# Stick-breaking attention in a decoder trunk: another order of the head loop, and the entry copies on VectorE

## The reference, cut to what matters

```python
def sb_block(q, k, v, q_pos, k_pos, bias):
    z = jnp.einsum('bqhd,bkhd->bhqk', q.astype(F32), k.astype(F32)) * (SB_HEAD_DIM ** -0.5)
    z = z + bias.astype(F32)[None, :, None, None]
    mask = k_pos[None, :] < q_pos[:, None]
    lb = jnp.where(mask, jax.nn.log_sigmoid(-z), 0.0)
    rev = lax.cumsum(lb, axis=3, reverse=True)
    after = jnp.concatenate([rev[..., 1:], jnp.zeros_like(rev[..., :1])], axis=-1)
    wgt = jnp.where(mask, jnp.exp(jax.nn.log_sigmoid(z) + after), 0.0)
    return jnp.einsum('bhqk,bkhd->bqhd', wgt, v.astype(F32)).astype(v.dtype)
```

## Time and profile before

| | |
|---|---|
| median of 3 executions | 2492.19 us (2490.45 to 2493.6) |
| the profiled execution | 2492.66 us, its span 2490.6 us |
| TensorE busy | 93% of the span |
| VectorE, ScalarE, GpSimd busy | 65%, 34%, 17% |
| span of stage A's projections and head loop | 425 to 745 us |
| chain that ended last, by engine | TensorE 70%, VectorE 14%, ScalarE 6%, GpSimd 4% |

### The profile page before, as it was taken

The page is one execution under the profiler, slowest core; times in us unless marked ns, Lnnn a source line. Parts: engine busy times, 40 slices in busy tenths (PEclk is TensorE's granted clock), DMA queues, the critical chain, the costliest instruction groups (busy, mean ns, idle before and its releaser), DMA issues.

```text
span 2490.6 us, 45870 instructions
## 1 busy us (share of the span) xinstructions
PE 2314.0 (93%) x18817; PEld 2209.6 (89%) x18817; DVE 1628.9 (65%) x1912; ACT 854.0 (34%) x1050; POOL 423.2 (17%) x323
## 2 busy tenths in 40 slices
PE   5999999986879999999999999989898977999998
PEld 5999999874559999999999999979787867999998
DVE  5666575677865757566757566777777758757573
ACT  5333232214333323234423233443433324423233
POOL 2000003590003000003000004061525264000002
PEclk8999999996889999999999999989999998999999
DMA  3242425572522142424142424243333322142422
GB/s 111 66 114 85 117 70 177 145 219 70 180 77 68 53 120 76 114 81 115 53 127 75 116 80 116 69 119 89 107 102 94 98 85 79 54 125 75 115 80 77
DMA packets 412887, 248.56 MB, mean 100 GB/s; under 512 B 12658, under 2 KB 387802, under 8 KB 412688
## 3 DMA queue, kind: packets, MB, share of 16 engines
q1 hardware_dynamic: 412279, 246.28, 34.7%
q10 hardware_dynamic: 460, 0.20, 0.0%
HBM read 232.48 MB, written 14.61 MB: 99 GB/s over the span
## 4 chain that ended last, share of the span: by engine, by line
PE 70%; DVE 14%; ACT 6%; POOL 4%; issue 3%; DMA 2%; SPq 1%; ACTq 0%; DVEq 0%; POOLq 0%
PE PS L239 45%; PE PS L744 16%; POOL prod L1133 2%; DVE wl L216 2%; PE PS L1344 2%; ACT wh L212 2%; PE PS L1291 1%; DVE xcs L2304 1%; PE PS L1224 1%; PE PS L2109 1%; DVE rstd L303 1%; DVE cbuf L1500 1%; PE PS L1235 1%; DVE xcs L2486 1%; DVE hl L285 1%
## 5 line engine op out<-in xcount | busy, mean ns | idle before, releaser
L239 PE MATMUL PS<-hh,wh 128*128 128x260 f32 (+1 forms) x2512 | 518.9, 288 | 33.2 <-DVE hl L285 12.8
L239 PE MATMUL PS<-hh,wl 128*128 128x260 f32 (+1 forms) x2512 | 510.6, 285 | 0.0
L239 PE MATMUL PS<-hl,wh 128*128 128x260 f32 (+1 forms) x2512 | 510.0, 285 | 0.0
L216 DVE TENSOR_TENSOR wl<-raw,wh 128x2048 fp32r<-128x2048 f32 (+2 forms) x187 | 345.0, 1845 | 153.8 <-ACT wh L212 152.4
L239 PEld LDWEIGHTS PS<-hh,wh 128*128 128x128 f32 (+1 forms) x2512 | 392.1, 191 | 47.5 <-issue 35.1
L239 PEld LDWEIGHTS PS<-hl,wh 128*128 128x128 f32 (+1 forms) x2512 | 391.7, 190 | 0.2
L239 PEld LDWEIGHTS PS<-hh,wl 128*128 128x128 f32 (+1 forms) x2512 | 391.5, 190 | 0.2
L212 ACT ACTIVATE wh<-raw 128x2048 fp32r<-128x2048 f32 (+2 forms) x187 | 266.5, 1425 | 302.7 <-PE PS L239 260.9
L276 POOL TENSOR_TENSOR sqr<-xT 128x520 f32 (+1 forms) x47 | 51.5, 1096 | 1631.0 <-DVE xT L915 1396.9
L239 PE MATMUL PS<-hid_h,wh 128*128 128x260 f32 x1408 | 285.4, 284 | 2.1 <-DVE hid_l L909 2.1
L239 PE MATMUL PS<-hid_h,wl 128*128 128x260 f32 x1408 | 283.9, 283 | 0.0
(11 more groups left out here) (357 smaller groups left out, 4556.3 us busy)
## 6 DMA issues: line engine op xcount, KB each, us to landing
raw<-in_ffn_gate_dram SPq DMA_DIRECT2D x88, 512.0 KB, 4.0
raw<-in_ffn_up_dram SPq DMA_DIRECT2D x88, 512.0 KB, 5.2
raw<-in_ffn_down_dram SPq DMA_DIRECT2D x128, 256.0 KB, 3.0
raw<-in_m_in_proj_dram SPq DMA_DIRECT2D x40, 512.0 KB, 5.3
raw<-in_ffn_down_dram SPq DMA_DIRECT2D x64, 192.0 KB, 2.6
page<-in_cache_sb_v_dram SPq DMA_DIRECT2D x48, 256.0 KB, 3.0
raw<-in_ab_in_proj_dram SPq DMA_DIRECT2D x20, 512.0 KB, 5.4
ms_b<-in_state_ssm_dram SPq DMA_DIRECT2D x32, 256.0 KB, 3.2
```

The costliest lines, as they stand in the source:

```text
L216: dve.tensor_tensor(wl[:, p, 0:cols], raw[:, p, 0:cols], wh[:, p, 0:cols].bitcast(F32), ALU.subtract).then_inc(w_ready, 1)
L239: ins = pe.matmul(out, x[:, k0, c:c + m], y[:, k, half * H2:(half + 1) * H2], start=k == 0 and a == 0, stop=k == nk - 1 and a == 2)
```

## The change

Entry: the last two v copies, the v row copy and the six page copies go from ScalarE to VectorE, where they stand behind the samples' bias step of iteration 0; TensorE makes all six page transposes before the loop. Loop: TensorE takes PV, then the scores of head `i` + 1, then the sums (in iteration 1 the scores come after the sums). ScalarE's `front` is parted into `softplus` and `z_copy`: for heads from 2 on, Abs, Exp and Ln stand ahead of the Exp that waits for t, and the z copy behind it. VectorE's convolution portions become 8, 17, then 5 and 12, and its half split moves to right behind t. The value units change places within the iterations (four in each of six iterations as before). Projection blocks: sample 0's query broadcast moves from behind block 2 to its middle, two reductions move to block 2, block 9 has 8 instead of 10 and evacuates at steps 0 and 3 instead of 2 and 7. The diff, cut to its core:

```diff
-            QS, ES, KS = 2, 3, 10
+            QS, ES, KS = 2, 2, 10
...
-                VROUNDS = [0] * 3 * NR + [0, 1, 0, 1, 0, 1, 0, 1, 0] * 6 + [0] * NR
+                VROUNDS = [0] * 3 * NR + 3 * [0, 0, 0, 1, 0, 1, 0, 1, 1, 0, 1, 0, 1, 0, 1, 0, 1, 0] + [0] * NR
...
                 def between(i):
-                    return [1] if i == QS + 1 else []
+                    return [i - QS] if i in (QS, QS + 1) else []
 
                 def after(i):
-                    return [0] if i == QS else [i - 1] if QS < i < B + 1 else []
-                REDUCES = [9] * (KS - ES - 1)
-                REDUCES.append(B * NPG - sum(REDUCES))
+                    return [i - 1] if QS < i < B + 1 else []
+                REDUCES = [[5, 6]] + [list(range(9))] * (KS - ES - 2)
+                REDUCES.append(list(range(B * NPG - sum(len(x) for x in REDUCES))))
+                STEPS = max(x[-1] for x in REDUCES) + 1
...
-                    sp.wait_ge(S["v_cp"], NB)
+                    sp.wait_ge(S["v_cp"], 2)
+                    sp.wait_ge(S["vt_cp"], NB - 2)
...
-                    pe.wait_ge(S["v_cp"], NB)
+                    pe.wait_ge(S["vt_cp"], NB - 2)
+                    for m in range(len(MISC)):
+                        misc(m)
                     for i in range(NH + 2):
-                        if i <= 1:
-                            for m in range(i * len(MISC) // 2, (i + 1) * len(MISC) // 2):
-                                misc(m)
-                        if 1 <= i <= NH:
-                            h = i - 1
-                            pe.wait_ge(S["sp_done"], h + 1)
...
-                                if n % 2:
-                                    values(i, n // 2)
                         if i >= 2:
...
                                 if kb % 2:
-                                    values(i, 5 + kb // 2)
+                                    values(i, kb // 2)
+                        if i + 1 < NH and i != 1:
+                            scores(i + 1)
+                        if 1 <= i <= NH:
+                            h = i - 1
+                            pe.wait_ge(S["sp_done"], h + 1)
...
+                                if n % 2:
+                                    values(i, 2 + n // 2)
+                        if i == 1:
+                            scores(2)
                         if i < NH:
                             values(i, 7)
                             values(i, 8)
-                        if i + 1 < NH:
-                            scores(i + 1)
...
-                    for k in range(2, NB):
-                        act.wait_ge(S["v_tr"], k + 1)
-                        act.activation(vtok[:, :, k * P:(k + 1) * P],
-                                       PS[:, 4 + k % 2, :].rearrange("p (t c) -> p t c", t=NTT), ACT.Copy)\
-                            .then_inc(S["v_cp"], 1)
-                    act.activation(vrow, PS[0:B, 6, :], ACT.Copy).then_inc(S["row_cp"], 1)
...
-                    def front(h):
+                    def softplus(h):
...
+                        if h < 2:
+                            z_copy(h)
+                        act.wait_ge(S["abs_done"], h + 1)
+                        act.activation(s, s, ACT.Exp, scale=-1.0).then_inc(S["e_done"], 1)
+                        act.wait_ge(S["e_done"], h + 1)
+                        act.activation(s, s, ACT.Ln, bias=1.0).then_inc(S["lnp_done"], 1)
+
+                    def z_copy(h):
+
                         if h >= 2:
                             act.wait_ge(S["t_done"], h - 1)
                         act.activation(zc2[:, h % 2, :], z_ps, ACT.Identity, scale=SCALE, bias=biasb[:, h:h + 1])\
                             .then_inc(S["z_cp"], 1)
...
                         if i == 0:
-                            front(0)
-                        if i <= 1:
-                            for m in range(i * len(MISC) // 2, (i + 1) * len(MISC) // 2):
...
-                        if 1 <= i <= NH:
-                            act.wait_ge(S["t_done"], i)
-                            w = sp_[:, (i - 1) % NSP, :]
-                            act.activation(w, w, ACT.Exp).then_inc(S["w_exp"], 1)
...
-                        if i + 1 < NH:
-                            front(i + 1)
-                        if i == 0:
+                            softplus(0)
                             act.wait_ge(S["dec"], 1)
...
+                        if i + 1 < NH and i != 1:
+                            softplus(i + 1)
+                        if i >= 3 and i % 2 == 1:
...
+                        if 1 <= i <= NH:
+                            act.wait_ge(S["t_done"], i)
+                            w = sp_[:, (i - 1) % NSP, :]
+                            act.activation(w, w, ACT.Exp).then_inc(S["w_exp"], 1)
+                        if i == 1:
+                            softplus(2)
+                        if 1 <= i < NH - 1:
+                            z_copy(i + 1)
...
-                        for r in range(max(REDUCES)):
-                            if i >= ES and r < REDUCES[i - ES]:
-                                reduce(sum(REDUCES[:i - ES]) + r)
-                            if r == 2:
+                        for r in range(STEPS):
+                            if i >= ES and r in REDUCES[i - ES]:
+                                reduce(sum(len(x) for x in REDUCES[:i - ES]) + REDUCES[i - ES].index(r))
+                            if r == (0 if i == KS - 1 else 2):
                                 evacuate(i, 0)
-                            if r == 7:
+                            if r == (3 if i == KS - 1 else 7):
                                 evacuate(i, 1)
...
+                            for k in range(2, NB):
+                                dve.wait_ge(S["v_tr"], k + 1)
+                                dve.tensor_copy(vtok[:, :, k * P:(k + 1) * P],
+                                                PS[:, 4 + k % 2, :].rearrange("p (t c) -> p t c", t=NTT))\
+                                    .then_inc(S["vt_cp"], 1)
+                            dve.tensor_copy(vrow, PS[0:B, 6, :]).then_inc(S["row_cp"], 1)
+                            for m, (kind, t) in enumerate(MISC):
+                                dve.wait_ge(S["misc_tr"], m + 1)
+                                dst, rows = {"k": (ktok[:, t, :], P), "tail": (tl, PADW + B), "krow": (krow, B)}[kind]
+                                dve.tensor_copy(dst, PS[0:rows, 6 + m % 2, :]).then_inc(S["misc_cp"], 1)
                             dve.wait_ge(S["dec"], 1)
...
-                        conv(5)
+                        conv(0 if i == 1 else 5)
                         if 1 <= i <= NH:
...
-                        conv(11)
+                        if i >= 3 and i % 2 == 1:
+                            pair = (i - 3) // 2
+                            dve.wait_ge(S["pv_hi"], pair + 1)
...
+                        conv(3 if i == 0 else 17 if i == 1 else 12)
...
-                        if i >= 3 and i % 2 == 1:
-                            pair = (i - 3) // 2
-                            dve.wait_ge(S["pv_hi"], pair + 1)
```

More of the change, by code:

```diff
@@ L1312, in _ @@
                                 if kb % 2:
-                                    values(i, 5 + kb // 2)
+                                    values(i, kb // 2)
[4 more added lines that the diff above has]
+                            pe.wait_ge(S["sp_done"], h + 1)
+                            if h >= 1:
+                                pe.wait_ge(S["t_done"], h)
+                            pieces = [(kb, kk) for kb in (0, 1, 3, 2) for kk in range(kb, NTT)]
+                            for n, (kb, kk) in enumerate(pieces):
+                                lo = KO[kb] + (kk - kb) * P
+                                ins = pe.matmul(s_ps[:, lo:lo + KW[kk]], (tri if kk == kb else ones)[:, :],
+                                                sp_[:, h % NSP, KO[kk]:KO[kk] + KW[kk]],
+                                                start=kk == kb, stop=kk == NTT - 1)
+                                if n == len(pieces) - 1:
+                                    ins.then_inc(S["sum_mm"], 1)
+                                if n % 2:
+                                    values(i, 2 + n // 2)
+                        if i == 1:
+                            scores(2)
                         if i < NH:
@@ L1420, in front @@
                             .then_inc(S["z_cp"], 1)
-                        act.wait_ge(S["abs_done"], h + 1)
-                        act.activation(s, s, ACT.Exp, scale=-1.0).then_inc(S["e_done"], 1)
-                        act.wait_ge(S["e_done"], h + 1)
-                        act.activation(s, s, ACT.Ln, bias=1.0).then_inc(S["lnp_done"], 1)
                     for i in range(NH + 2):
@@ L1601, in _ @@
                                               ALU.subtract).then_inc(S["t_done"], 1)
[L1602 removed]
+                        if i >= 3 and i % 2 == 1:
+                            pair = (i - 3) // 2
```

(11 more changed lines are left out.)

22 lines of the change are left out of this document (4 added, 18 removed).

## The result

The changed kernel takes 2477.3 us (median of four runs, 2475.4 to 2479.3), the kernel before 2491.6 beside it (2490.5 to 2493.6): ratio 0.9941, 95% interval 0.9925 to 0.9957. That is faster, by 14.3 us at the median. The forecast was 2479.9.

What follows compares the result with a forecast made beforehand. It took the head-loop entry and the loop, where VectorE and TensorE wait for each other once per head, as the bounds. Entry -14.9, loop +5.7 and tail -3.6 gave -12.8: 2492.66 to 2479.9 us, range 2469 to 2487.

Steps and rivals of the forecast that it cites:

- Projection blocks: Key products on GpSimd before the head loop: last product 1.0 us earlier, at 557.2; head 0's scores start at 553.6.
- Entry on ScalarE: Head 0's first softplus, with copies gone from ScalarE: Abs starts at 557.2, Ln ends at 562.2 instead of 572.36.
- Entry on VectorE and t(0): Nine copies on VectorE until 567.6, slow TensorE clock; first zc minus suffix sums, t(0), at 579.0, 14.9 us earlier.
- rival (a): Full clock at the entry and no page waits: t(0) 574.0, loop 123.5, 22.9 us saved, about 2470; chance 0.18.
- The loop: Head loop from t(0) to t(7): 128.6 us against 122.9, so 5.7 longer, with 12.4 of waits.
- TensorE's chain of 15.1: TensorE's path per head from t: t and Exp 2.8, PV 2.5, scores 2.85, suffix sums 6.86; 15.1 us.
- The tail: After t(7): the layer norm's first mean follows the sums at once, 0.2 us before t(7), saving 3.6.
- The sum: Whole change: -14.9 at the entry, +5.7 in the loop, -3.6 in the tail, -12.8 us in all.
- rival (c): TensorE's clock falls in every head, making PV and scores slow: up to 20 us lost, 2500; chance 0.06.
- signs of being wrong: Stated failures: t(0) later than 585, a loop interval above 21 us, or PV slow in most heads.
- (d): Entry starts no earlier, through a later last product and slow scores: t(0) 585, sum -6.8, 2485.9 us; chance 0.10.
- (b): Loop waits stay 16.85 us and 10.2 of extra convolution come on top: -8.3, 2484.4 us; chance 0.16.

Runs made afterwards that it cites:

- 36 of them: Changed kernel plus unread TensorE work: four full-row matmuls ahead of iteration 3's value product, 36 transposes ahead of iteration 8's; 2473.1 us in one run.
- the run with 64 rows: Changed kernel plus unread 64-row matmuls in TensorE's idle time ahead of the value products of iterations 3 and 8; 2472.9 us, ratio 0.9924.
- the second trace: The changed kernel itself run and traced once more, nothing altered; 2477.2 us against 2491.3 for the kernel before, ratio 0.9935.

## Why the prediction held, step by step

- **Projection blocks.** Last product forecast to end at 557.2, ended at 556.8; scores of head 0 forecast at 553.6, started at 553.3. Against the stage's start that is 1.1 earlier, forecast 1.0. The sum is right by two errors that cancel: the products ahead of the page wait ended at 530.6 instead of 535.0 (the starts of the rows less their waits), 4.1 earlier against the stage's start where 1.8 was forecast, and the wait for pages grew by 2.2 and not by 1.4 at most, with another 0.85 lost in the products behind it.
- **Entry on ScalarE.** Abs at 556.9 and Ln done at 561.9, forecast 557.2 and 562.2. Right.
- **Entry on VectorE and t(0).** Forecast 579.0, came at 575.5 and 573.4: the failed step. The copies were done at 566.5 and 564.5 (forecast 567.6 at the slow clock, 565.2 at the full one), but the scores of head 1 took 2.62 and 2.42, not 4.60. I had read "busy with scores and transposes and still 0.50" as a sign that this work leaves the clock low, and took the slow clock to 573; by the earlier trace rows the scores had ended at 561.77, and the stretch held mask products and transposes. The runs show that transposes need not leave it low: 36 of them held the clock as matmuls do, and in the run with 64 rows it came back at about 562.5 while TensorE did page transposes alone. The Trainium skill says in "TensorE: Matmul & The Clock Gate", Part 4: PE-mode transpose, that a transpose doesn't count as work for the clock the same way; the value product of 2.37 us behind 4.15 us of transposes speaks against it here, and the measurement decides. The rival (a)'s t(0), 574.0, was the right one; its other half, no page waits, wasn't.
- **The loop.** Forecast 128.6; measured 132.6 and 129.1. Interval by interval the first trace agrees with the forecast where VectorE sets it (22.7, 18.4 and 16.2, as forecast), and where pages and a slow value product do (t(4) to t(5), 19.9 against 20.2). t(1) to t(2) is 4.1 too long there, and 17.1 against a forecast 17.2 in the second trace; t(2) to t(3), a page wait and a slow value product, is 19.6 and 19.4 against 18.4; t(6) to t(7) is 14.6 and 16.0 against 15.5. TensorE's chain of 15.1 adds up to 15.0 from its terms; no interval hangs on it. The balance also holds: ten more microseconds of convolution behind t(0), against waits of VectorE that fell from 16.85 to 13.1 in the second trace, make +6.4; measured is +6.2.
- **The tail.** From t(7) to the output it was 733.03 - 716.80 = 16.2 before and is 720.75 - 708.14 = 12.6 after, in both traces: -3.6, as forecast.
- **The sum.** Forecast -12.8; in the stage it was -12.0 in one execution (t(0) 3.2 better than forecast, the loop 4.0 worse) and -17.1 in the other (t(0) 4.7 better). The medians say -14.3 and -14.1. The first trace's near agreement is of two errors that cancel: the clock at the entry, and the clock in iteration 3. The -14.3 lies between the two traces, but which value of the stage is typical was not measured more finely than by these two. Nor does what follows the stage move as a block, as the forecast had it: it differs by 5.6 us among the four traces of the two kernels (1754.7 to 1760.3), so a single time agrees with the sum partly by luck.

The rival (c), a fall of the clock in every head, came true in part: of eight value products four were slow in the first trace (iterations 3, 4, 6 and 8, 3.33 to 4.53 against 2.37) and five in the second (iteration 2 as well). Two of them the forecast had counted. The rival's price of 3.9 a head was paid in full only in t(1) to t(2) of the first trace (4.1); in iteration 2 the slow one cost nothing, t(0) to t(1) being 22.7 in both traces, because VectorE's own queue ended last. So two of the forecast's signs of being wrong appeared, a loop interval above 21 (21.3 in the first trace, beside its own 22.7) and slow value products in most heads (the second trace), and the time held all the same. (d) didn't happen. (b), waits that don't shrink, is the first trace's balance to the letter (16.6 us of waits), and yet only one execution's.

## What to carry to other kernels

Taking work off an engine ahead of a joint and reordering behind it can be worth more together than apart: here the new order alone cost 4 us and paid 5 to 6 once the entry was free. Look at what the engine would do in the time that is freed; if its queue has nothing ready, moved work only lands later. Before a stretch of one trace is explained, take a second trace: in the two of the changed kernel TensorE's clock fell and rose at other moments, and single intervals moved by 4 us while the whole span moved by 0.9.

## What the runs showed of the hardware

The same entry ran at half clock for about 10 us in one execution of the same program (rows above, 556 to 566) and for 3.4 in the next. The Trainium skill says in "TensorE: Matmul & The Clock Gate", Part 1: The HAM clock gate, that the moment of the change varies from run to run; the two traces agree. It gives half a microsecond for sustained matmuls; here, with idle time and transposes among them, the clock came back some 7 us apart. Stretches of the second execution and of the run with 64 rows (columns as above):

```profile
555.50:558.00 2.50, 2.50 (x14) 2.42 (x13) 1.86 (x4) 1.53 (x2) 1.36 (x2) 0.50 0.00 0
...
559.00:560.00 1.00, 0.18 (x2) 0.21 (x3) 0.72 (x2) 1.00 (x2) 0.00 (x0) 1.00 0.00 0
```

```profile
558.00:559.00 1.00, 0.00 (x0) 0.00 (x0) 1.00 (x2) 1.00 (x2) 0.00 (x0) 1.00 0.00 0
...
559.50:562.00 2.50, 2.50 (x12) 2.03 (x12) 1.38 (x2) 2.44 (x4) 0.00 (x0) 0.50 0.97 369
...
563.00:564.00 1.00, 0.91 (x7) 0.57 (x8) 0.96 (x2) 0.00 (x0) 0.00 (x0) 1.00 0.00 0
```

In the run with 64 rows TensorE is granted the full clock up to 559, the low one from 559.5 to 562.5, and the full one again from 563, with page transposes as its only work from 559.27 on. What else decides when it returns wasn't settled: the kernel before stays low from about 553 to 590 in both its traces, through scores, transposes and pauses of up to 5.7 us. That an idle stretch can make the work behind it nearly twice as long (4.53 against 2.37), and that matmuls with 128 or 64 rows and transposes avoid it alike, is what the traces of iteration 8 show, with one trace for each form.
